# Nine taps of two convolution chunks as diagonal matrices on TensorE, a new VectorE order, and the turning inside the projection

## The chip, the cores and the metric

The kernel is one program on one core of one Trainium2 chip. The metric is the device time of one execution in microseconds; smaller is better. All inputs and outputs are 32-bit floats.

## What is computed

Four transformer layers run one after the other on a sequence of 256 positions with 1024 features: two layers of a first block, two of a second. The change touches one sublayer only, the "even mixer" of the second block's first layer, called the hybrid mixer in the kernel. Its core, from the reference:

```python
def even_mixer(h, w_in, w_out, dw_w, dw_b, ln_g, ln_b):
    """Stick-breaking attention heads || Conformer conv channels. h: (B,S,D)."""
    proj = h @ w_in
    q, k, v, u, gate = jnp.split(
        proj, [SB_WIDTH, 2 * SB_WIDTH, 3 * SB_WIDTH, 3 * SB_WIDTH + CONV_CH], axis=-1)
    a_out = merge_heads(stick_breaking_attention(
        split_heads(q, SB_HEADS), split_heads(k, SB_HEADS), split_heads(v, SB_HEADS)))
    c = u * jax.nn.sigmoid(gate)
    c = causal_depthwise_conv(c, dw_w, dw_b)
    c = jax.nn.silu(layer_norm(c, ln_g, ln_b))
    return jnp.concatenate([a_out.astype(h.dtype), c], axis=-1) @ w_out
```

There are 8 heads of 64 features and 512 convolution channels; the convolution is depthwise, causal, with 31 taps. A head's weights are `exp(log_sigmoid(z) + rest)`, where `rest` is a reversed running sum of `log_sigmoid(-z)` over the keys.

## The kernel before

**Tiling.** 128 partitions; positions come as two blocks of 128 (`NTB = 2`), features as chunks of 128. Weight slabs of 1 MB come through a ring of four slots. For a slab, SyncE loads `raw[s]`, ScalarE rounds it into `w_hi[s]` (`high_one`, L551), and VectorE, or GpSimd (L474), subtracts to get `w_lo[s]` (`low_one`, L1155, which signals `slab_ready`). A product is three passes, `three` (L1802 to L1804): hi by hi, and the two cross terms. Products whose operands are plain 32-bit floats (heads, triangles) are one call each, and stand in the trace as two MATMUL records; a transpose is one record. SyncE loads the next slab of a slot once its `slab_ready` says that `raw[s]` was read.

**Order.** Every engine has a program of its own, written out by hand, and semaphores tie them. In the hybrid mixer they are:

- TensorE: the slabs of the input projection, with heads 0 to 3 between them. The slab that gives the last keys (`slab_into(7, 3)`) is copied out by ScalarE (`evacuate(3, words(1536, 512), ..., bank=7)`, L570). Then `all_copied`, the logits of heads 4 to 7 (`stick_logits`, L2261 to L2264), values of heads 2 and 3, 18 warm matmuls on zeros (`keep_warm`, L1882), running sums of heads 4 to 7 (`stick_rest`, L2272 to L2274), 4 warm ones, values of heads 4 to 7 (`stick_values`, L2283 to L2285), 8 warm ones. Then `project_out` over chunks 0 to 3 (the heads' half; block 0, then block 1; 48 matmuls), `conv_turned` (L2293: the convolution, channels on partitions, is transposed into banks 6 and 7, positions on partitions), 16 warm ones, a wait for the layer norm, 8 transposes back (L2331), 8 warm ones, and `project_out` over chunks 4 to 7.
- VectorE: 124 taps of the convolution (4 chunks by 31; L1666 and L1669) in pieces given by `convolve(n)`, with everything else between them: `low_one`, `bounds` (L1675: a minimum of the logits, which releases ScalarE's exponential), `softplus` (L1683, which releases `stick_rest`), `low_of_banks` (L1461). After the turning: statistics (L1737), mean and variance (L1740), `1/std` (L1744), the scaling (L1746).
- ScalarE: `high_one` for the slabs, the copies out of PSUM, exp and log of a head (`softplus_logs`, L937 and L940), the weights (`stick_weights`, L947), and after the scaling SiLU (L990) and rounding (L986) of each chunk, before the second half of the output projection.

The slots 0 to 3 of the output projection hold its rows in that order: chunks 0 to 3 need slots 0 and 1, chunks 4 to 7 need slots 2 and 3.

Of the kernel before, what the change touches and what calls it, by code (L numbers as in the profile page):

```python
# [23 lines left out]
ACT = mybir.ActivationFunctionType  # L24
# [21 lines left out]
TOP_K = 64  # L46
SB_HEADS = 8
CONV_TAPS = 31
GATE_RANK = 16
GLA_TAU = 16.0  # L50
SOFTPLUS_EDGE = 20.0
CONV_CHUNKS = 4
TAPS_AHEAD, TAPS_BETWEEN = 64, 8
BUCKETS = 32
MAX_DIST = 128
# [77 lines left out]
def build(nc, A, out):  # L133
    with ExitStack() as ctx:
# [3 lines left out]
        def sem(name):  # L138
            return ctx.enter_context(nc.semaphore(name))
# [39 lines left out]
        def words(a, n):  # L179
            return arena[:, a:a + n]  # L180
# [44 lines left out]
        def col(name, i=0):  # L225
            c = row_of[name] + i
            return cols[:, c:c + 1]
# [44 lines left out]

        sb_z, sb_min, sb_ln, sb_sp, sb_rest, sb_w, sb_pv = (
            sem("sb_z"), sem("sb_min"), sem("sb_ln"), sem("sb_sp"), sem("sb_rest"), sem("sb_w"), sem("sb_pv"))
        cv_tap, cv_turn, cv_ms, cv_std, cv_norm, cv_back, cv_silu = (
            sem("cv_tap"), sem("cv_turn"), sem("cv_ms"), sem("cv_std"), sem("cv_norm"), sem("cv_back"), sem("cv_silu"))
        stored = sem("stored")
# [52 lines left out]
        def hyb_views():  # L330
            return dict(
                q=words(0, 1024).rearrange("p (c t) -> p c t", t=SEQ), k_all=words(1024, 1024),
                k=words(1024, 1024).rearrange("p (c t) -> p c t", t=SEQ),
                gate=words(3072, 1024).rearrange("p (s c t) -> p s c t", s=2, t=SEQ),
                v=proj[:, 8:10, :], pad=words(5120, 4 * (SEQ + CONV_TAPS - 1)).rearrange("p (c t) -> p c t", c=4),
                co=words(6400, 1024).rearrange("p (c t) -> p c t", t=SEQ), cs=words(7424, 1024).rearrange("p (c t) -> p c t", t=SEQ),
                l=words(8448, 1536).rearrange("p (b n) -> p b n", b=4),
                sp=words(9984, 1536).rearrange("p (b n) -> p b n", b=4), w=words(11520, 1536).rearrange("p (b n) -> p b n", b=4))

        def halves(t, m):  # L340

# [127 lines left out]
        def _(pool):  # L469
# [62 lines left out]
            for s, n in ((0, 3), (1, 3), (2, 1), (3, 4)):  # L532
                ring.skip(s, n)
            low_one(2)
            ring.skip(2, 2)
            ffn_elsewhere(3)


# [1 line left out]
        def _(act):  # L540
# [12 lines left out]
            def high_one(slot, dmas=1):  # L553
                high(slot, *ring.take(slot, dmas))
# [12 lines left out]
            def evacuate(s, dst, scale=1.0, func=ACT.Copy, bank=None):  # L567

                act.wait_ge(slab_used[s], ring.uses[s] + 1)
                ins = act.activation(dst, ps[:, 4 + s if bank is None else bank, :], func, scale=scale).then_inc(proj_free[s], 1)  # L570
                made[s] += 1
                return ins

            def preload(func, at=154):

                act.activation(small[:, at:at + 1], eps_col, func)
# [335 lines left out]
            for l in range(2):  # L912
# [13 lines left out]
                if l == 0:  # L926
# [40 lines left out]
                    evacuate(2, words(512, 512), bank=6)  # L967
                    stick_weights(1)
                    high_one(2)
                    evacuate(3, words(1536, 512), 64 ** -0.5, bank=7)  # L970
                    softplus_logs(2, 2)
                    stick_weights(2)
                    stick_weights(3)
                    high_one(3)
                    act.wait_ge(sb_pv, SB_HEADS)
                    for b in range(2):
                        act.activation(x_hi[:, 2 * b:2 * b + 2, :].rearrange("p c t -> p (c t)"), ps[:, 4 + b, :], ACT.Copy)\
                            .then_inc(x_hi_done, 1)
                    preload(ACT.Sqrt)
                    act.wait_ge(cv_ms, 1)  # L980
                    act.activation(ln_std, ln_mv.rearrange("p (b s) -> p b s", s=2)[:, :, 1], ACT.Sqrt, bias=eps_col)\
                        .then_inc(cv_std, 1)
# [55 lines left out]
        def _(dve):  # L1038
# [112 lines left out]
            def low_one(slot):  # L1151

                u, _ = lows.take(slot)
                dve.wait_ge(hi_done[slot], u + 1)
                dve.tensor_tensor(w_lo[slot][:, :], raw[slot][:, :], w_hi[slot][:, :].bitcast(F32), ALU.subtract)\  # L1155
                    .then_inc(slab_ready[slot], 1)
# [476 lines left out]
            for l in range(2):  # L1633
                ffn(False, 0, 2 + 2 * l)
                after_ffn(2 + 2 * l, ("norm_g_2", l * 6 + 2), True, 2 if l == 0 else None)
                if l == 0:
# [15 lines left out]
                        dve.wait_ge(proj_free[u_slot], made[u_slot] + 1)  # L1652

                    last_tap = {}
                    taps = [(k, 2 * half + c) for half in range(2) for k in range(CONV_TAPS) for c in range(2)]

                    def convolve(n):
                        for _ in range(n):
# [27 lines left out]
                    def bounds(pair):  # L1686
                        stick_bound(2 * pair)
                        stick_bound(2 * pair + 1)
# [25 lines left out]
                        made[s] += 1  # L1714
                    convolve(CONV_TAPS * 2 - (3 + 2 + 9 + 7 + 6 + 5 + 12))
                    gated_half(1, 0, 1)
                    low_one(0)
                    low_one(1)
                    convolve(16)
                    low_one(2)  # L1720
                    bounds(2)
                    bounds(3)
                    convolve(11)
                    softplus(2)
                    softplus(3)
                    convolve(16)
                    low_of_banks(2)
                    convolve(CONV_CHUNKS * CONV_TAPS)
                    low_one(3)
                    for s in (2, 3):  # L1730
                        used[s] += 2
                        made[s] += 2
                    dve.wait_ge(cv_tap, CONV_CHUNKS * CONV_TAPS)

                    dve.wait_ge(cv_turn, 1)
                    for tb in range(NTB):
                        ins = dve.bn_stats(ln_stats[:, 6 * tb:6 * tb + 6], ps[:, 6 + tb, :])  # L1737
# [7 lines left out]
                    for tb in range(NTB):  # L1745
                        dve.tensor_scalar(xn[:, tb, 0:512], ps[:, 6 + tb, :], ln_mv[:, 2 * tb:2 * tb + 1], ln_rstd[:, tb:tb + 1],  # L1746
                                          ALU.subtract, ALU.mult).then_inc(cv_norm, 1)
                    for c in range(4):
                        dve.wait_ge(x_hi_done, want(x_hi_done))
                        dve.tensor_tensor(x_lo[:, 4 + c, :], hyb["cs"][:, c, :], x_hi[:, 4 + c, :].bitcast(F32), ALU.subtract)\  # L1750
                            .then_inc(x_ready, 1)
# [44 lines left out]
        def _(pe):  # L1796
# [437 lines left out]
            for l in range(2):  # L2234
                turn_block(0)
                if l == 0:
# [40 lines left out]
                    def stick_values(hd):  # L2277
# [7 lines left out]
                        pe.matmul(o[:, P:SEQ], v1, w[:, SEQ:3 * P], start=False, stop=True, skip_group_check=True)\  # L2285
                            .then_inc(sb_pv, 1)

                    def conv_turned():

                        pe.wait_ge(cv_tap, CONV_CHUNKS * CONV_TAPS)  # L2290
                        for tb in range(NTB):
                            for c in range(4):
                                ins = pe.transpose(ps[:, 6 + tb, c * P:c * P + P], hyb["co"][:, c, tb * P:tb * P + P], ident)  # L2293
                        ins.then_inc(cv_turn, 1)

# [16 lines left out]
                    heads(stick_logits, 2)  # L2312
                    heads(stick_logits, 3)
                    heads(stick_values, 1)
                    keep_warm(18)
                    heads(stick_rest, 2)
                    heads(stick_rest, 3)
                    keep_warm(4)
                    heads(stick_values, 2)
                    heads(stick_values, 3)  # L2320
                    keep_warm(8)

                    base = x_new(6)
                    project_out(HYB_OUT, lambda tb, k: base + k // 2 + 1, ks=range(4))
                    conv_turned()
                    keep_warm(16, 4)
                    pe.wait_ge(cv_norm, NTB)
                    for c in range(4):
                        for tb in range(NTB):
# [58 lines left out]
```

## Time and profile before

| | |
|---|---|
| runs | 1711.65, 1714.98 (median), 1716.35 us |
| the profiled execution | 1709.17 us, span 1707.4 us |
| mean granted TensorE clock | 0.994 of full speed |
| busy | TensorE 97%, VectorE 70%, ScalarE 51%, GpSimd 7% |

All times below are microseconds from the start of the span. The hybrid mixer lies between about 884 and 997. A timeline row gives start, length (for several instructions together from the first start to the last end), engine, line, operation, tiles and count; brackets give the idle time before it and what ended it. The length of a matmul's record contains the pipeline, so that matmuls in a row overlap: the pace is read from start to start.

### The profile page before, as it was taken

How to read it: one execution, taken by the hardware profiler on the slowest of the kernel's cores; microseconds unless marked ns; L12 is line 12 of the kernel's file. 1: busy time of each engine (PE TensorE's matmuls, PEld its weight loads, DVE VectorE, ACT ScalarE, POOL GpSimd, SP SyncE). 2: the span in 40 equal slices, each digit the busy share in tenths (PEclk: the TensorE clock that was granted, in tenths of full speed). 3: DMA queues.
4: the chain of work that ended last, by engine and by line, in shares of the span. 5: the costliest groups of instructions: out<-in, count | busy, mean ns of one | idle time of the engine just before them, and what ended most of it. 6: DMA issues, size and time to landing. Idle time of an engine off the chain costs nothing. (4 is left out here: it accounts for less than half of the span.)

```text
span 1707.4 us, 26142 instructions
## 1 busy us (share of the span) xinstructions
PE 1654.7 (97%) x10075; PEld 1454.3 (85%) x10084; DVE 1197.4 (70%) x1773; ACT 863.0 (51%) x1207; POOL 116.1 (7%) x36
## 2 busy tenths in 40 slices
PE   7999999989999998999999999999999999999998
PEld 6998988879798887888889788888988889888887
DVE  2796778777668788566669966667666675676665
ACT  6323655563665556544466374446544465364443
POOL 5351000012600000000010000000000000000000
PEclk9999999999999999999999999999999999999999
DMA  8623366745245555555644235555555653345552
GB/s 267 217 75 100 124 216 192 222 133 164 69 152 173 197 177 192 161 197 173 220 148 161 94 113 177 195 184 185 174 183 196 199 182 128 124 136 177 192 189 82
DMA packets 220065, 283.44 MB, mean 166 GB/s; under 512 B 13004, under 2 KB 197315, under 8 KB 219987
## 3 DMA queue, kind: packets, MB, share of 16 engines
q1 hardware_dynamic: 218499, 278.18, 50.1%
q10 hardware_dynamic: 1488, 4.17, 0.8%
q8 instruction: 55, 0.90, 0.2%
q14 instruction: 23, 0.19, 0.0%
HBM read 280.88 MB, written 1.44 MB: 165 GB/s over the span
## 5 line engine op out<-in xcount | busy, mean ns | idle before, releaser
L1971 PE MATMUL ps<-x_pair,w_hi 128*128 128x512 f32 x1728 | 612.1, 398 | 0.0
L551 ACT ACTIVATE w_hi<-raw 128x2048 fp32r<-128x2048 f32 x262 | 498.2, 1909 | 132.9 <-PE ps L1973 92.2
L1234 DVE TENSOR_TENSOR w_lo<-raw,w_hi 128x2048 fp32r<-128x2048 f32 x162 | 371.1, 2291 | 195.4 <-ACT w_hi L551 195.4
L1973 PE MATMUL ps<-x_pair,w_lo 128*128 128x256 f32 x1728 | 485.1, 281 | 0.0
L1971 PEld LDWEIGHTS ps<-x_pair,w_hi 128*128 128x128 f32 x1728 | 324.7, 188 | 80.2
L1973 PEld LDWEIGHTS ps<-x_pair,w_lo 128*128 128x128 f32 x1728 | 326.3, 189 | 2.1
L1802 PE MATMUL ps<-w_hi,x_pair 128*128 128x256 f32 (+2 forms) x672 | 215.8, 321 | 19.6 <-DVE x_pair L1090 10.9
L1804 PE MATMUL ps<-w_hi,x_pair 128*128 128x256 f32 (+2 forms) x672 | 210.7, 314 | 0.0
L1803 PE MATMUL ps<-w_lo,x_pair 128*128 128x256 f32 (+2 forms) x672 | 210.6, 313 | 0.0
L1155 DVE TENSOR_TENSOR w_lo<-raw,w_hi 128x2048 fp32r<-128x2048 f32 x74 | 171.9, 2331 | 38.0 <-ACT w_hi L551 37.9
L1802 PE MATMUL ps<-w_hi,g_hi 128*128 128x512 f32 x480 | 188.7, 393 | 0.0
L1804 PE MATMUL ps<-w_hi,g_lo 128*128 128x512 f32 x480 | 187.7, 391 | 0.0
L1803 PE MATMUL ps<-w_lo,g_hi 128*128 128x512 f32 x480 | 187.2, 390 | 0.0
L1802 PE MATMUL ps<-x_pair,w_hi 128*128 128x256 f32 (+1 forms) x640 | 183.5, 287 | 2.5 <-POOL w_lo L474 2.2
L1803 PE MATMUL ps<-x_pair,w_hi 128*128 128x256 f32 (+1 forms) x640 | 181.6, 284 | 0.0
L1804 PE MATMUL ps<-x_pair,w_lo 128*128 128x256 f32 (+1 forms) x640 | 181.5, 284 | 0.0
L1802 PEld LDWEIGHTS ps<-w_hi,x_pair 128*128 128x128 f32 x672 | 129.6, 193 | 31.3 <-issue 14.2
L1261 DVE TENSOR_REDUCE arena<-ps 128x256 f32<-128x512 f32 x216 | 142.0, 684 | 12.3 <-PE ps L1973 10.0
L474 POOL TENSOR_TENSOR w_lo<-raw,w_hi 128x2048 fp32r<-128x2048 f32 x21 | 100.1, 4784 | 743.4 <-ACT w_hi L551 743.4
L1804 PEld LDWEIGHTS ps<-w_hi,x_pair 128*128 128x128 f32 x672 | 129.7, 193 | 7.1
L1803 PEld LDWEIGHTS ps<-w_lo,x_pair 128*128 128x128 f32 x672 | 129.9, 193 | 6.7
L1802 PEld LDWEIGHTS ps<-x_pair,w_hi 128*128 128x128 f32 (+1 forms) x640 | 122.6, 192 | 5.5 <-POOL w_lo L474 2.8
(181 smaller groups left out, 1847.2 us busy)
## 6 DMA issues: line engine op xcount, KB each, us to landing
raw<-in_ffn_w_in SPq DMA_DIRECT2D x88, 1024.0 KB, 5.1
raw<-in_ffn_w_up SPq DMA_DIRECT2D x44, 1024.0 KB, 5.1
raw<-in_ffn_w_out SPq DMA_DIRECT2D x44, 1024.0 KB, 4.9
raw<-in_ffn_w_down SPq DMA_DIRECT2D x22, 1024.0 KB, 5.3
raw<-in_hgrn_w_in SPq DMA_DIRECT2D x16, 1024.0 KB, 5.8
raw<-in_gla_w_in SPq DMA_DIRECT2D x12, 1024.0 KB, 5.3
raw<-in_hyb_w_in SPq DMA_DIRECT2D x10, 1024.0 KB, 5.5
raw<-in_dsa_w_in SPq DMA_DIRECT2D x6, 1024.0 KB, 5.7
```

The costliest lines, as they stand in the source:

```text
L474: pool.tensor_tensor(w_lo[slot][:, :], raw[slot][:, :], w_hi[slot][:, :].bitcast(F32), ALU.subtract)\
L551: act.activation(w_hi[slot][:, :], raw[slot][:, :], ACT.Copy).then_inc(hi_done[slot], 1)
L1155: dve.tensor_tensor(w_lo[slot][:, :], raw[slot][:, :], w_hi[slot][:, :].bitcast(F32), ALU.subtract)\
L1234: dve.tensor_tensor(w_lo[slot][:, :], raw[slot][:, :], w_hi[slot][:, :].bitcast(F32), ALU.subtract)\
L1261: dve.tensor_reduce(ff_u[:, b, g, :], halves_of, AX_X, ALU.add).then_inc(part_sum[g][b], 1)
L1802: pe.matmul(out_ap, a_hi, b_hi, start=start, stop=False, skip_group_check=True)
L1803: pe.matmul(out_ap, a_hi, b_lo, start=False, stop=False, skip_group_check=True)
L1804: return pe.matmul(out_ap, a_lo, b_hi, start=False, stop=stop, skip_group_check=True)
L1971: pe.matmul(ps[:, bank, :].rearrange("p (x t) -> p x t", x=2), w_hi[s][:, at:at + P], x_pair[:, :, k, :], start=k == 0, stop=False, skip_g ...
L1973: ins = pe.matmul(ps[:, bank, 0:SEQ], w_lo[s][:, at:at + P], x_hi[:, k, :], start=False, stop=k == NK - 1, skip_group_check=True)
```

## The change

Of the 31 taps, the last nine (k = 22 to 30) of channel chunks 2 and 3 go to TensorE. ScalarE writes 18 matrices of 128 by 128, the identity times a column of tap weights (`diag`, in free words of `arena`). TensorE multiplies a window of `pad` by each, for both blocks, straight into banks 6 and 7, which is where the turned convolution goes: the stationary operand is [channels, positions], the moving one the diagonal matrix, so the product comes out turned. These 36 products stand in three of the places of warm matmuls. `conv_turned` then adds VectorE's share of chunks 2 and 3 by a product with the identity, and transposes chunks 0 and 1; it stands inside the first half of the output projection, ahead of block 1, chunk 1. VectorE does 106 taps. Its two subtractions for slots 0 and 1 stand behind `bounds` of heads 4 to 7; that for slot 2 goes to GpSimd, which waits for the last tap; that for slot 3 stands behind the layer norm's scaling. ScalarE's rounding of slot 3 stands behind the copies of the heads' output.

```diff
+PE_TAPS = 9
+VECTOR_TAPS = CONV_CHUNKS * CONV_TAPS - 2 * PE_TAPS
+PE_TAP_LIST = [(k, c) for k in range(CONV_TAPS - PE_TAPS, CONV_TAPS) for c in (2, 3)]
...
@@ GpSimd
-            ring.skip(2, 2)
+            ring.skip(2, 1)
+            pool.wait_ge(cv_tap, VECTOR_TAPS)
+            low_one(2)
@@ ScalarE
                     stick_weights(1)
                     high_one(2)
+                    for j, (k, c) in enumerate(PE_TAP_LIST):
+                        act.activation(hyb["diag"][:, j, :], ident, ACT.Copy, scale=col("conv_dw_w_2", k * 4 + c))\
+                            .then_inc(diag_done, 1)
                     evacuate(3, words(1536, 512), 64 ** -0.5, bank=7)
...
-                    high_one(3)
                     act.wait_ge(sb_pv, SB_HEADS)
...
                     preload(ACT.Sqrt)
+                    high_one(3)
@@ VectorE
-                    taps = [(k, 2 * half + c) for half in range(2) for k in range(CONV_TAPS) for c in range(2)]
+                    taps = [(k, 2 * half + c) for half in range(2) for k in range(CONV_TAPS - half * PE_TAPS) for c in range(2)]
...
                     gated_half(1, 0, 1)
+                    convolve(24)
+                    bounds(2)
+                    bounds(3)
                     low_one(0)
                     low_one(1)
-                    convolve(16)
-                    low_one(2)
-                    bounds(2)
-                    bounds(3)
-                    convolve(11)
+                    lows.skip(2, 1)
                     softplus(2)
                     softplus(3)
-                    convolve(16)
+                    convolve(12)
                     low_of_banks(2)
                     convolve(CONV_CHUNKS * CONV_TAPS)
-                    low_one(3)
...
-                    dve.wait_ge(cv_tap, CONV_CHUNKS * CONV_TAPS)
                     dve.wait_ge(cv_turn, 1)
... (behind the scaling, L1746)
+                    low_one(3)
@@ TensorE
+                    def conv_taps(n):
+                        for _ in range(n):
+                            j, (k, c) = diagonals.pop(0)
+                            pe.wait_ge(diag_done, j + 1)
+                            for tb in range(NTB):
+                                pe.matmul(ps[:, 6 + tb, c * P:c * P + P], hyb["pad"][:, c, k + tb * P:k + tb * P + P],
+                                          hyb["diag"][:, j, :], start=j == 0, stop=False, skip_group_check=True)
...
-                        pe.wait_ge(cv_tap, CONV_CHUNKS * CONV_TAPS)
+                        pe.wait_ge(cv_tap, VECTOR_TAPS)
                         for tb in range(NTB):
-                            for c in range(4):
+                            for c in (2, 3):
+                                pe.matmul(ps[:, 6 + tb, c * P:c * P + P], hyb["co"][:, c, tb * P:tb * P + P], ident,
+                                          start=False, stop=True, skip_group_check=True)
+                            for c in range(2):
                                 ins = pe.transpose(ps[:, 6 + tb, c * P:c * P + P], hyb["co"][:, c, tb * P:tb * P + P], ident)
...
                     heads(stick_values, 1)
-                    keep_warm(18)
+                    conv_taps(11)
                     heads(stick_rest, 2)
                     heads(stick_rest, 3)
-                    keep_warm(4)
+                    conv_taps(4)
                     heads(stick_values, 2)
                     heads(stick_values, 3)
-                    keep_warm(8)
+                    conv_taps(3)
+                    keep_warm(2, 0)
...
-                    project_out(HYB_OUT, lambda tb, k: base + k // 2 + 1, ks=range(4))
-                    conv_turned()
-                    keep_warm(16, 4)
+                    project_out(HYB_OUT, lambda tb, k: base + k // 2 + 1, {(1, 1): conv_turned}, range(4))
+                    keep_warm(8, 4)
                     pe.wait_ge(cv_norm, NTB)
```

## Rows read from the trace of the kernel before

**Rows 1.** The page's part 1: busy us (share of the span) xinstructions of each engine.
```profile
PE 1654.7 (97%) x10075; PEld 1454.3 (85%) x10084; DVE 1197.4 (70%) x1773; ACT 863.0 (51%) x1207; POOL 116.1 (7%) x36
```

**Rows 2.** TensorE's timeline, 965 to 987: first projection half, turning, warm matmuls, second half.
```profile
965.93 1.67 PE L1882 MATMUL ps<-const 128*128 128x512 bf16 x7 [0.16 <-issue]
967.82 0.47 PE L1802 MATMUL ps<-w_hi,x_pair 128*128 128x512 f32 x1 [0.22 <-DVE x_pair L1461]
...
978.82 1.03 PE L2293 MATMUL ps<-const,arena 128*128 128x128 f32 x8
979.91 3.40 PE L1882 MATMUL ps<-const 128*128 128x512 bf16 x15
983.69 1.09 PE L2331 MATMUL ps<-const,xn 128*128 128x128 f32 x8 [0.38 <-DVE xn L1746]
984.62 1.89 PE L1882 MATMUL ps<-const 128*128 128x512 bf16 x8
986.31 0.47 PE L1802 MATMUL ps<-w_hi,x_pair 128*128 128x512 f32 x1
```

**Rows 3.** VectorE's timeline, 966 to 984: heads' low parts, last taps, the layer norm.
```profile
966.99 1.28 DVE L1461 TENSOR_TENSOR x_pair<-ps,x_pair 128x512 fp32r<-128x512 f32 x2
968.19 7.60 DVE L1669 SCALAR_TENSOR_TENSOR arena<-arena,cols 128x256 f32<-128x256 f32 x19
...
979.96 1.29 DVE L1737 BATCH_NORM_STATS2 small<-ps 128x6 f32<-128x512 f32 x2 [1.97 <-PE ps L2293]
...
982.10 1.53 DVE L1746 TENSOR_SCALAR xn<-ps,small 128x512 f32<-128x512 f32 x2
```

**Rows 4.** TensorE's timeline, 938 to 964: logits, values, warm matmuls, running sums.
```profile
947.93 0.67 PE L2261 MATMUL ps<-arena 64*128 64x256 f32 x2 [0.89 <-ACT arena L570]
...
953.21 0.71 PE L2264 MATMUL ps<-const 128*128 128x128 f32 x4
953.85 0.43 PE L2283 MATMUL ps<-arena 128*64 128x128 f32 x2
...
955.16 3.83 PE L1882 MATMUL ps<-const 128*128 128x512 bf16 x17 [0.16 <-issue]
959.40 0.70 PE L2272 MATMUL ps<-arena,const 128*128 128x256 f32 x2 [0.41 <-DVE arena L1683]
...
963.01 1.03 PE L1882 MATMUL ps<-const 128*128 128x512 bf16 x4
963.97 0.43 PE L2283 MATMUL ps<-arena 128*64 128x128 f32 x2
```

**Rows 5.** ScalarE's timeline: around the copy of the last keys.
```profile
941.72 1.91 ACT L551 ACTIVATE w_hi<-raw 128x2048 fp32r<-128x2048 f32 x1
947.08 0.60 ACT L570 ACTIVATE arena<-ps 128x512 f32<-128x512 f32 x1 [3.45 <-PE ps L1804]
```

**Rows 6.** ScalarE's timeline, 999 to 1001: scaled copies of 128 columns from PSUM.
```profile
999.04 2.17 ACT L627 ACTIVATE x_pair<-ps,cols 128x128 fp32r<-128x128 f32 x8 [1.31 <-PE ps L1890]
```

**Rows 7.** The same line of ScalarE over the span: duration ns min/median/max, first and last start.
```profile
L627 ACT ACTIVATE x_pair<-ps,cols x184: 343/382/482, 11.3 to 1520.8; 128x128 fp32r<-128x128 f32 x176, 128x256 fp32r<-128x256 f32 x8
```

**Rows 8.** TensorE's timeline, 72 to 77: 32 records of 32-bit products in a row.
```profile
72.94 3.74 PE L2053 MATMUL ps<-arena 128*128 128x128 f32 x32
76.43 0.36 PE L1802 MATMUL ps<-w_hi,x_pair 128*128 128x256 f32 x1
```

**Rows 9.** VectorE's timeline, 938 to 955: slots 0 and 1, the last bound.
```profile
938.18 4.50 DVE L1155 TENSOR_TENSOR w_lo<-raw,w_hi 128x2048 fp32r<-128x2048 f32 x2
...
953.96 0.56 DVE L1675 TENSOR_SCALAR arena<-ps 128x384 f32<-128x384 f32 x1 [0.93 <-PE ps L2264]
```

**Rows 10.** GpSimd's timeline: its one subtraction in this mixer.
```profile
890.68 4.61 POOL L474 TENSOR_TENSOR w_lo<-raw,w_hi 128x2048 fp32r<-128x2048 f32 x1 [429.74 <-ACT w_hi L551]
```

**Rows 11.** Stretches behind the mixer: busy time and records of each engine, clock, DMA.
```profile
998.00:1001.00 3.00, 1.87 (x13) 1.69 (x14) 2.14 (x7) 1.96 (x8) 0.00 (x0) 0.95 0.00 0
1001.00:1004.00 3.00, 3.00 (x16) 3.00 (x16) 2.96 (x10) 2.97 (x7) 0.00 (x0) 0.50 0.00 0
```

More of the change, by code:

```diff
@@ L274, in build @@
             sem("sb_z"), sem("sb_min"), sem("sb_ln"), sem("sb_sp"), sem("sb_rest"), sem("sb_w"), sem("sb_pv"))
+        diag_done = sem("diag_done")
         cv_tap, cv_turn, cv_ms, cv_std, cv_norm, cv_back, cv_silu = (
@@ L337, in hyb_views @@
                 l=words(8448, 1536).rearrange("p (b n) -> p b n", b=4),
-                sp=words(9984, 1536).rearrange("p (b n) -> p b n", b=4), w=words(11520, 1536).rearrange("p (b n) -> p b n", b=4))
+                sp=words(9984, 1536).rearrange("p (b n) -> p b n", b=4), w=words(11520, 1536).rearrange("p (b n) -> p b n", b=4),
+                diag=words(13056, 2 * PE_TAPS * P).rearrange("p (j n) -> p j n", n=P))
         def halves(t, m):
@@ L2286, in stick_values @@
                             .then_inc(sb_pv, 1)
+                    diagonals = list(enumerate(PE_TAP_LIST))
+                    def conv_taps(n):
[5 more added lines that the diff above has]
+                                          hyb["diag"][:, j, :], start=j == 0, stop=False, skip_group_check=True)
                     def conv_turned():
-                        pe.wait_ge(cv_tap, CONV_CHUNKS * CONV_TAPS)
+                        pe.wait_ge(cv_tap, VECTOR_TAPS)
                         for tb in range(NTB):
-                            for c in range(4):
+                            for c in (2, 3):
+                                pe.matmul(ps[:, 6 + tb, c * P:c * P + P], hyb["co"][:, c, tb * P:tb * P + P], ident,
+                                          start=False, stop=True, skip_group_check=True)
+                            for c in range(2):
                                 ins = pe.transpose(ps[:, 6 + tb, c * P:c * P + P], hyb["co"][:, c, tb * P:tb * P + P], ident)
```

## The prediction

> **What bounds the kernel now.** I read the page's head first: TensorE is busy for 97% of the span [rows 1], at a mean clock of 0.994. So a change is worth what it takes out of TensorE's own row of work, or out of its waits, and what it puts in counts in full. The page's chain of waits explains too small a share of the span to help here, so I went to the timelines of the one stage that the diff touches, first TensorE's, then the engines that release it.
>
> Two things are to be seen in TensorE's timeline at the end of the mixer [rows 2]. The first half of the output projection runs from 967.82 to 978.82 without a gap: 48 matmuls in 11.00 us, 0.229 each. The turning follows, 1.09 us to the next start. Then TensorE does nothing useful from 979.91 to 983.69 (3.78 us of warm matmuls and a short wait), because the layer norm must first be made: VectorE starts its statistics at 979.96 and has the scaled block at 982.10 + 1.53 = 983.63 [rows 3]. From the transposes back (983.69) to the second half (986.31) it is another 2.62 us, which the change leaves alone. VectorE had the last tap done at 968.19 + 7.60 = 975.79 [rows 3], 3.0 us before TensorE came to the turning. The taps do not hold the turning at its present place; they would, at 974.7, if it stood 18 matmuls earlier. That is why the taps and the turning move together.
>
> Earlier in the stage TensorE is held once by ScalarE (the copy of the last keys at 947.08, after which the logits start at 947.93) and once, by 0.41 us, by VectorE's softplus at 959.40 [rows 4, 5].
>
> **The change part by part.** I count along TensorE from the logits of head 4 to the transposes back, since there each step starts when the one before is issued.
>
> *The 18 diagonal matrices on ScalarE.* They stand behind the rounding that ends at 941.72 + 1.91 = 943.63 and ahead of the copy of the last keys. ScalarE was idle for 3.45 us there [rows 5]: that is their cover. Their price isn't in the trace. The nearest row is the scaled copy of 128 columns: 8 in 2.17 us with a record of 0.38 at the end, so (2.17 - 0.38) / 7 = 0.256 from start to start [rows 6, 7]. [...] From below: the rounding of 2048 columns out of SBUF takes 1.91 [rows 5], 0.12 for every 128 columns. I take 0.256, the row of the same size with a scale by partition: 18 x 0.256 = 4.6 us, so the copy begins at about 948.2 in place of 947.08, **+1.1 us**. Ends: 0.12 gives 2.2 us, inside the cover, and 0.0; the record's whole length of 0.38, if nothing overlapped, gives 6.8 us and +3.4, but the row itself overlaps, so I weigh this end little. What is queued behind the matrices on ScalarE is this copy and then the exponentials, and TensorE's `all_copied` waits for the copy, so the logits are late by all of it: their start goes to 949.0.
>
> The row says 0.256 for a copy with a scale from a column. The Trainium skill, ScalarE: Activation LUTs, section "What ACT_TABLE_LOAD costs", says that an ACTIVATE with immediates takes 186 ns + 0.833 ns per element, that each pointer operand adds about 93 ns, and that neighbours overlap by about 93 ns. As an estimate from that page one matrix is 186 + 93 + 107 - 93 = 293 ns, 18 are 5.3 us, and the sum below would be 0.7 us higher. It speaks against the change, but only by that much.
>
> *Bounds and softplus on VectorE.* The last bound is at 953.96 and waits for TensorE [rows 9], so it goes to 955.1. Its follower is now the pair of subtractions for slots 0 and 1 (4.50 us together [rows 9]), in place of 11 taps: bound done 955.6, subtractions to 960.1. Softplus is of the bound's size, 0.56, so head 4's is done at about 960.6. ScalarE's exponential and logarithm go beside that and are as late as the logits. TensorE, see the next step, comes at 961.1: its wait of 0.41 us for softplus is gone, and VectorE has 0.5 us to spare. In exchange VectorE idles: 24 taps at 7.60 / 19 = 0.40 [rows 3] end at about 947.9, and the first new bound is possible at about 950.7. This costs nothing as long as the last 8 taps are in time, which I check below.
>
> *Eleven taps in place of 18 warm matmuls.* A tap is two products of 128 x 128 x 128 in 32-bit floats, each two records. The trace has such a row with both operands in `arena`: 32 records from 72.94 to 76.43, 0.109 each [rows 8]. A tap is 4 x 0.109 = 0.436, 11 are 4.80 us. The stretch that they replace lasts from 955.16 to 959.40, 4.24 us, wait included [rows 4]. **+0.56 us**.
>
> *Four taps in place of 4 warm matmuls.* 1.74 us in place of 963.97 - 963.01 = 0.96 [rows 4]. **+0.78 us**. ScalarE's last weights are ready before that, so nothing was hidden by it.
>
> *Three taps and 2 warm matmuls in place of 8.* 1.31 + 2 x 0.22 + 0.16 of issue = 1.9 us against 967.82 - 965.93 = 1.89 [rows 2]. **0.0 us**. The copies of the heads' output and `low_of_banks` go on beside it. Today the first low part starts at 966.99, 3.0 us behind the first value product, and TensorE waits 0.22 us for it [rows 2 to 4]; VectorE will then be idle and not in the middle of taps, so this stays covered.
>
> *The turning.* Four of its eight transposes become products of two records: 12 x 0.109 = 1.31 in place of 1.09. **+0.22 us**. Does it have to wait? Adding up, the values start at 963.97 + 1.1 + 0.56 + 0.78 = 966.4 and the projection at 967.82 + 2.44 = 970.3. The turning stands behind 30 of its 48 matmuls, 30 x 0.229 = 6.9, at 977.1. VectorE starts `low_of_banks` 3.0 us behind the values as now, at 969.4, and has it done 1.28 later [rows 3], at 970.7; 8 taps of 0.40 follow, last tap 973.9. That is 3.2 us early. The 18 taps that VectorE is rid of were worth 7.2 us to it and buy TensorE nothing directly.
>
> *The layer norm behind the projection.* From the turning's first start to the statistics it was 979.96 - 978.82 = 1.14, now 1.4; the statistics start at 978.5 and the scaled block is there 3.67 us later [rows 3], at 982.2. TensorE meanwhile does the remaining 18 matmuls: 977.1 + 1.31 + 18 x 0.229 = 982.5. Here the gain is found: the norm is hidden completely. But 8 warm matmuls still stand between, 986.31 - 984.62 = 1.69 us [rows 2], and they run although the block is ready. So the stretch of 3.78 us becomes 1.7. **-2.1 us**, not -3.8.
>
> *Slot 2 on GpSimd, slot 3 late.* GpSimd's subtraction takes 4.61 [rows 10], from 973.9 to 978.5; slot 3 on VectorE runs from 982.2 to 984.4. Both are needed only by the second half, after 986: cover of 2 us and more. SyncE's next loads for slots 0 and 1 are let go some 17 us later than now, at 958 and 960, and those for 2 and 3 at 978 and 984.4; the feed-forward part rounds slots 0 and 1 after 987, and slots 2 and 3 after 1002. A slab lands in some 5 us, so none of them is late. **0.0 us**; if this cover failed, a late slab would cost its overhang directly.
>
> *Sum.* 1.1 + 0.56 + 0.78 + 0.0 + 0.22 - 2.1 = **+0.6 us**, on the profiled execution's 1709.17: 1709.8. The profiled execution is 5.8 us under the median of the three runs; the stage's terms do not depend on that, so I put them on the median: 1714.98 + 0.6 = **1715.6 us**. The bounds of the matrices alone move it from -0.5 to +4.0, where the upper end holds no overlap on ScalarE at all.
>
> **The rivals.**
> *A, the clock falls once more.* TensorE's gap ahead of the logits grows from 0.89 to 2.0 us. Behind the mixer a stretch of 3 us in which TensorE is busy for only 1.87 us stands ahead of one of 3 us at a granted clock of 0.50, that is 1.2 GHz instead of 2.4 [rows 11]. If the same happens at the logits, a stretch of 3 us does the work of 1.5: +1.5, together +2.1 us, 1717.1. Against it: the mean clock of 0.994 leaves room for 0.006 x 1707.4 / 0.5 = 20 us at half clock in the whole span, so that such stretches are few; and the one at 1001 could as well vanish by a shift.
>
> *B, a net gain.* The matrices stay inside the 3.45 us of cover (0.19 each decides), the logits start as now: -0.5. If besides the 3 us at 0.50 behind the mixer do not come, another -1.5: -2.0 us, 1713.0. For it: the shift changes the moment of that gap. That it would be more is excluded by the 8 warm matmuls and the 1.3 us that the taps add on TensorE in any case.
>
> *C, slower beyond the bound.* The taps don't run at 0.109 a record but like the logits' short products, which read `const` on both sides: 4 records from 953.21 to 953.85, 0.16 each [rows 4]. The windows of `pad` start at any word, which no row of the trace shows for a stationary operand. Then 72 + 8 records cost 80 x 0.051 = 4.1 us more, all on TensorE's row: +4.7 us, 1719.7, and with matrices of 0.30 (5.4 us, +0.8 on the taken value) +5.5, 0.32%. It decides from about 0.16 a record on. Against it: the row of 32 is the same kind of product, on the same tile.
>
> *D, the turning waits for the last tap.* For this VectorE would have to be 3.2 us later than worked out; it has no new work in that stretch. 2 in 100.
>
> **How the numbers follow.** Forecast 0.55, A 0.18, B 0.18, C 0.07, D 0.02. About 0.3% (5.1 us) is what a measurement of this kernel can tell from no change. All cases but part of C and D lie within it, and the before runs themselves spread over 4.7 us, which can carry a small difference across: faster 0.04, same 0.90, slower 0.06. The range takes B and C with some of the scatter of the runs: 1710 to 1721 us.
>
> **What would show it right or wrong.** In the profile of the changed kernel: 18 copies on ScalarE at about 0.26 from start to start, and the copy of the last keys behind them without an idle time; a gap of about 2 us ahead of the first logits; taps at 0.109 a record; no wait of TensorE at the turning; a second projection half that starts within 1 us of 986.3. The prediction is wrong if the taps run slower than 0.12 a record, if a wait for VectorE stands ahead of the running sums or the turning, if the gap at the scaled block is larger than the 8 warm matmuls, or if the stretches of low clock differ in number.

## The result and the profile after

The changed kernel takes 1722.1 us in the median of 20 runs (1715.88 to 1724.35), the one before 1715.4 us (20 runs, 1709.15 to 1718.66). The ratio is 1.0035, with a 95% interval of 1.0024 to 1.0045: **slower by 0.35%, some 6 us**. The forecast was +0.6 us, 1715.6, in a range of 1710 to 1721; the median lies 1.1 us above that range.

I begin with the stretches of TensorE's timeline in which the two differ. The views by stretches give busy time and records of TensorE, its weight loads, VectorE, ScalarE and GpSimd, then the granted clock and the DMA share and rate. The kernel before:

```profile
944.00:956.00 12.00, 10.95 (x74) 9.00 (x74) 10.60 (x22) 3.53 (x6) 0.00 (x0) 1.00 0.62 203
956.00:968.00 12.00, 11.22 (x74) 7.34 (x74) 12.00 (x30) 9.42 (x14) 0.00 (x0) 1.00 0.01 3
```

The changed kernel (all of its stage is some 5 us later in this execution; see the experiment before_again for that):

```profile
944.00:956.00 12.00, 9.42 (x73) 8.76 (x69) 8.63 (x22) 8.53 (x22) 0.00 (x0) 1.00 0.01 1
956.00:968.00 12.00, 12.00 (x53) 9.91 (x52) 6.09 (x6) 5.29 (x10) 0.00 (x0) 0.57 0.03 7
```

The clock is the news: 0.57 in the mean from 956 to 968, that is at 0.50 (1.2 GHz) for 10.2 us in the record of the clock. TensorE is "busy" for the whole of it, yet issues only 53 records in place of 74 (the kinds of work in the two windows are not all the same; like rows are compared below). TensorE's timeline of the changed kernel, the answer to rows 4:

```profile
954.62 0.67 PE L2268 MATMUL ps<-arena 64*128 64x256 f32 x2 [2.58 <-ACT arena L577]
...
956.09 0.70 PE L2268 MATMUL ps<-arena 64*128 64x256 f32 x2
956.62 0.38 PE L2269 MATMUL ps<-arena 64*128 64x128 f32 x2
956.93 1.16 PE L2271 MATMUL ps<-const 128*128 128x128 f32 x4
958.02 1.22 PE L2268 MATMUL ps<-arena 64*128 64x256 f32 x2
...
960.74 1.22 PE L2268 MATMUL ps<-arena 64*128 64x256 f32 x2
...
963.47 0.69 PE L2290 MATMUL ps<-arena 128*64 128x128 f32 x2
...
965.43 6.04 PE L2302 MATMUL ps<-arena 128*128 128x128 f32 x44
971.31 0.60 PE L2279 MATMUL ps<-arena,const 128*128 128x256 f32 x2
```

The first head of these logits takes 956.09 - 954.62 = 1.47 us, the third 960.74 - 958.02 = 2.72: the clock falls in the second. Ahead of the first stands the idle gap of 2.58 us, where [rows 4] had 0.89. ScalarE's timeline shows what made it (answering [rows 5]): 18 matrices from 948.52 to 953.78, 0.29 apart and not 0.256, and the copy of the last keys right behind them, without idle time:

```profile
946.72 1.91 ACT L558 ACTIVATE w_hi<-raw 128x2048 fp32r<-128x2048 f32 x1
948.52 5.37 ACT L978 ACTIVATE arena<-const,cols 128x128 f32<-128x128 f32 x18
953.78 0.58 ACT L577 ACTIVATE arena<-ps 128x512 f32<-128x512 f32 x1
```

At the end of the stage everything is as forecast. VectorE (answering [rows 3]) has its last tap at 980.38 + 3.25 = 983.63 and waits 5.03 us for the turning, not the other way round, and the block is ready at 990.80 + 1.53 = 992.3; TensorE (answering [rows 2]) issues the rest of the first half until 992.81 and then 8 warm matmuls that nobody needs:

```profile
980.38 3.25 DVE L1679 SCALAR_TENSOR_TENSOR arena<-arena,cols 128x256 f32<-128x256 f32 x8
988.65 1.30 DVE L1743 BATCH_NORM_STATS2 small<-ps 128x6 f32<-128x512 f32 x2 [5.03 <-PE ps L2313]
...
990.80 1.53 DVE L1752 TENSOR_SCALAR xn<-ps,small 128x512 f32<-128x512 f32 x2
```

```profile
992.81 1.67 PE L1889 MATMUL ps<-const 128*128 128x512 bf16 x7
994.33 1.04 PE L2351 MATMUL ps<-const,xn 128*128 128x128 f32 x8
```

**One ledger for all traces.** I measured the same six stretches on TensorE in every trace, from start to start, from the values of head 0 (one slab of the input projection before the gap) to the second half of the output projection. The table is worked out from the timelines; "hold" runs to the logits of head 4, and the last stretch contains the turning, the norm and the transposes back.

| kernel | hold | logits | to the sums | to the values | to the projection | to the 2nd half | total |
|---|---|---|---|---|---|---|---|
| before | 9.73 | 5.92 | 5.55 | 4.57 | 3.85 | 18.49 | 48.1 |
| before_again | 9.73 | 5.92 | 5.54 | 4.57 | 3.85 | 18.46 | 48.1 |
| changed | 11.42 | 8.85 | 7.84 | 5.40 | 3.41 | 16.77 | 53.7 |
| after_again | 11.43 | 9.90 | 8.35 | 5.39 | 3.42 | 16.79 | 55.3 |
| fill | 11.44 | 5.93 | 6.09 | 5.39 | 3.41 | 16.79 | 49.1 |
| early | 9.73 | 5.93 | 6.08 | 5.40 | 3.41 | 16.80 | 47.4 |
| held | 11.42 | 8.81 | 6.79 | 4.46 | 3.31 | 18.55 | 53.3 |
| hold_15 | 10.55 | 5.92 | 6.09 | 5.39 | 3.42 | 16.80 | 48.2 |
| taps_only | 9.73 | 5.93 | 6.09 | 5.39 | 3.41 | 18.99 | 49.5 |
| turn_only | 9.73 | 5.93 | 5.53 | 4.58 | 3.85 | 15.76 | 45.4 |
| early_trim | 9.77 | 5.93 | 6.09 | 5.39 | 3.41 | 15.06 | 45.7 |
| seven | 9.74 | 5.92 | 5.59 | 4.60 | 3.42 | 15.06 | 44.3 |

The change adds 53.7 - 48.1 = 5.6 us to the stage in the profiled execution, which at 1723.8 us is one of the slower of the 20; the times say some 6 us. What is open at this point is why the clock falls.

### The profile page after: what moved, and what is told of

It reads as the page before. It is cut to its first block and busy times, and to the rows that moved or that the text cites. A ratio compares the mean times of both kernels' runs of the same rounds, so it can differ in the third digit from the quotient of the medians.

```text
span 1722.0 us, 26222 instructions
## 1 busy us (share of the span) xinstructions
PE 1666.7 (97%) x10116; PEld 1469.3 (85%) x10124; DVE 1189.3 (69%) x1754; ACT 868.3 (50%) x1225; POOL 120.6 (7%) x37
## 3 DMA queue, kind: packets, MB, share of 16 engines
q1 hardware_dynamic: 218499, 278.18, 49.5%
## 5 line engine op out<-in xcount | busy, mean ns | idle before, releaser
L1809 PE MATMUL ps<-w_hi,x_pair 128*128 128x256 f32 (+2 forms) x672 | 218.8, 326 | 19.1 <-DVE x_pair L1100 10.6
L1811 PE MATMUL ps<-w_hi,x_pair 128*128 128x256 f32 (+2 forms) x672 | 213.3, 317 | 0.0
L479 POOL TENSOR_TENSOR w_lo<-raw,w_hi 128x2048 fp32r<-128x2048 f32 x22 | 104.6, 4773 | 831.8 <-ACT w_hi L558 748.4
L1809 PEld LDWEIGHTS ps<-w_hi,x_pair 128*128 128x128 f32 x672 | 131.8, 196 | 30.5 <-issue 13.1
L1811 PEld LDWEIGHTS ps<-w_hi,x_pair 128*128 128x128 f32 x672 | 132.0, 196 | 7.4
```

What stands on the lines that cost most here:

```text
L479: pool.tensor_tensor(w_lo[slot][:, :], raw[slot][:, :], w_hi[slot][:, :].bitcast(F32), ALU.subtract)\
L1809: pe.matmul(out_ap, a_hi, b_hi, start=start, stop=False, skip_group_check=True)
L1811: return pe.matmul(out_ap, a_lo, b_hi, start=False, stop=stop, skip_group_check=True)
```

## The experiments

**The changed kernel again, for a second trace.** No edit.

> The changed kernel unaltered, for a second trace of it. Theory 'clock': the granted clock is 0.50 for about 10 us from the logits of head 4 on again, and the ratio is 1.003 to 1.004 again. Rival 'chance': the fall at that place was the luck of one execution; then this trace has full clock between the logits and the running sums, and the loss has to be looked for elsewhere.

Ratio 1.0026 (1.0012 to 1.0040), a little under the 1.003 to 1.004 that I expected. The fall is there again, after the same gap of 2.58 us, and lasts 13.7 us this time; the stage takes 55.3 us. It is not the luck of one execution. This trace too is of one of the longer executions (1722.8 us), and whether all executions have the fall, two traces can't say; the times are looked at under hold_15.

**The gap filled with warm matmuls.**

```diff
                     slab_into(7, 3)
+                    keep_warm(10, 0)
                     all_copied()
                     heads(stick_logits, 2)
```

> The changed kernel with 10 warm matmuls into bank 0 between the last slab of keys and the wait for its copy, so that TensorE isn't idle for the 2.6 us ahead of the logits; nothing waits longer (10 x 0.216 = 2.2 us). Theory 'clock': the clock stays at 1.0 through logits and taps, the stage is some 4 to 5 us shorter than in the changed kernel, ratio to before 1.000 to 1.001. Rival 'work': the taps and VectorE's order cost the time themselves; then the ratio stays at 1.003 or above.

Ratio 1.0007 (0.9997 to 1.0016). TensorE's timeline:

```profile
952.54 2.33 PE L1889 MATMUL ps<-const 128*128 128x512 bf16 x10
955.30 0.67 PE L2268 MATMUL ps<-arena 64*128 64x256 f32 x2 [0.43 <-ACT arena L577]
...
961.23 0.43 PE L2290 MATMUL ps<-arena 128*64 128x128 f32 x2
...
962.30 5.18 PE L2302 MATMUL ps<-arena 128*128 128x128 f32 x44
967.32 0.60 PE L2279 MATMUL ps<-arena,const 128*128 128x256 f32 x2
```

The logits start as late as in the changed kernel, 11.44 us after the values of head 0, but they run at full clock, and the stage is 4.6 us shorter than the changed kernel's and 6.2 us shorter than its second trace. Ten matmuls that compute nothing take back nearly all of the loss. The 18 matrices stand in their old place here and hold the copy as long, so they do no harm of their own beyond the hold. "Clock" holds, "work" falls.

**The matrices made early.** `diagonals(n)` makes the next n of the 18 (its definition is left out).

```diff
                     high_one(3)
                     for s in range(2):
                         evacuate(s, hyb["v"][:, s, :], bank=s)
                         high_one(s)
+                    diagonals(9)
                     evacuate(2, words(0, 512), bank=6)
                     high_one(2)
+                    diagonals(9)
                     evacuate(3, words(1024, 512), 64 ** -0.5, bank=7)
...
                     high_one(2)
-                    for j, (k, c) in enumerate(PE_TAP_LIST):
-                        act.activation(hyb["diag"][:, j, :], ident, ACT.Copy, scale=col("conv_dw_w_2", k * 4 + c))\
-                            .then_inc(diag_done, 1)
                     evacuate(3, words(1536, 512), 64 ** -0.5, bank=7)
```

> The changed kernel with the 18 matrices made some 35 us earlier on ScalarE, 9 ahead of and 9 behind the copy of the second query slab, in its idle times there. The copy of the last keys is then on time, and TensorE's gap ahead of the logits is 0.9 us as before the change. Theory 'clock': no fall there, and the 1.7 us of the hold are gone too: ratio 0.999 to 1.000. Rival 'work': ratio 1.002 to 1.003, only the hold's 1.7 us less than the changed kernel.

Ratio 0.9992 (0.9982 to 1.0001), the stage at 47.4. Hold and fall are both gone. This is what the parts of the change are worth without them: 48.1 - 47.4 = 0.7 us in the trace. The times alone can't tell it from the kernel before, since the interval reaches 1.0001.

**Only the hold: the kernel before, with the matrices made in the changed kernel's place and not used.** The constants, the semaphore and the tile that this needs are left out of the cut.

```diff
                     stick_weights(1)
                     high_one(2)
+                    for j, (k, c) in enumerate(PE_TAP_LIST):
+                        act.activation(hyb["diag"][:, j, :], ident, ACT.Copy, scale=col("conv_dw_w_2", k * 4 + c))\
+                            .then_inc(diag_done, 1)
                     evacuate(3, words(1536, 512), 64 ** -0.5, bank=7)
```

> The kernel before with the 18 matrices made on ScalarE at the changed kernel's place, and used by nobody: only the hold of the copy. Theory 'clock': TensorE's gap ahead of the logits is 2.6 us, the clock falls at the logits, but the 18 warm matmuls behind them bring it back sooner than the taps do: 1.7 us for the hold and 2 to 4 us for the clock, ratio 1.002 to 1.003. Rival 'the taps pull the clock down': full clock here, +1.7 us alone, ratio 1.001.

Ratio 1.0034 (1.0021 to 1.0048) from six runs, above the 1.002 to 1.003 that I expected, and as much as the whole change. The stretches:

```profile
944.00:956.00 12.00, 9.42 (x77) 8.79 (x74) 12.00 (x19) 8.52 (x22) 0.00 (x0) 1.00 0.54 176
956.00:968.00 12.00, 12.00 (x46) 8.59 (x47) 6.20 (x14) 4.86 (x9) 0.00 (x0) 0.57 0.27 88
```

And TensorE's timeline:

```profile
955.11 0.67 PE L2268 MATMUL ps<-arena 64*128 64x256 f32 x2 [2.58 <-ACT arena L574]
...
963.92 0.69 PE L2290 MATMUL ps<-arena 128*64 128x128 f32 x2
...
965.89 4.98 PE L1889 MATMUL ps<-const 128*128 128x512 bf16 x18
970.71 0.59 PE L2279 MATMUL ps<-arena,const 128*128 128x256 f32 x2
```

The same gap, the same fall of 10.2 us, without a tap on TensorE and with all warm matmuls in place. So neither the taps nor the missing warm matmuls pull the clock down. That the 18 warm ones would end the fall sooner than the taps did not show: it lasts 10.2 us here, 10.2 and 13.7 us in the two traces with taps. Its price was lower, though: of 53.3 - 48.1 = 5.2 us the hold is 1.7, which leaves 3.5 us for the fall, within the 2 to 4 expected, against 4.7 in the changed kernel.

**The hold without the gap: the same kernel with 10 warm matmuls ahead of the wait.** The edits are those of held and of fill together.

> The kernel before with the 18 unused matrices in the changed kernel's place on ScalarE, and the 10 warm matmuls into bank 0 ahead of the wait: the hold without the idle gap. Theory 'clock': full clock at the logits, and what is left is the hold alone, +1.7 to 2.1 us, ratio 1.001. Rival 'the matrices hurt otherwise' (by a shared port, or the table reload): ratio stays at the 1.0034 of the held kernel.

Ratio 1.0005 (0.9995 to 1.0014). The hold of 1.7 us alone would be 1.0010, inside the interval; the fall is needed for the 1.0034. There is no trace of this kernel that can be compared; that the clock stays up here rests on the times, and on the mean clocks of the runs, 0.990 to 0.992 against 0.985 to 0.989 in held.

**The kernel before again, for a second trace.** No edit.

> The kernel before unaltered, for a second trace of it: which of the stretches of low clock outside the mixer are its own. Ratio 1.000, and its interval says what this comparison can tell apart. All theories of the mixer expect full clock between the slab of the last keys and the running sums.

Ratio 0.9995 (0.9985 to 1.0006). The stage takes 48.1 us as in the first trace, though it begins 5.1 us later in the span (values of head 0 at 943.28 in place of 938.20). The record of the clock has more low stretches ahead of the mixer here than in the first trace, and they lie at the same places as in the traces of the changed kernel. So the 5 us by which the changed kernel's stage is later in its profile are none of the change's doing, and the two profiled executions, 1709.17 and 1723.8 us, exaggerate the difference. The prediction wanted to be called wrong if the stretches of low clock differ in number; that sign says nothing, since they differ between two traces of one kernel (five in the first, six in this).

**Fifteen matrices in place, three early: a gap in between.**

```diff
+                    diagonals(3)
                     evacuate(2, words(0, 512), bank=6)
                     high_one(2)
...
                     high_one(2)
-                    for j, (k, c) in enumerate(PE_TAP_LIST):
-                        act.activation(hyb["diag"][:, j, :], ident, ACT.Copy, scale=col("conv_dw_w_2", k * 4 + c))\
-                            .then_inc(diag_done, 1)
+                    diagonals(15)
                     evacuate(3, words(1536, 512), 64 ** -0.5, bank=7)
```

> The changed kernel with 15 of its 18 matrices in their place and 3 made early: the copy of the last keys is held by some 0.8 us in place of 1.7, TensorE's gap ahead of the logits is about 1.7 us, between the 0.9 without a fall and the 2.6 with one. If the gap's length alone decides and 1.7 us is short enough: full clock there, ratio 1.000 to 1.001. If it is long enough: the fall of 10 us again, ratio 1.002 to 1.003. Falls in some executions only would show as two clusters of times.

Ratio 1.0007 (0.9998 to 1.0016).

```profile
954.11 0.67 PE L2274 MATMUL ps<-arena 64*128 64x256 f32 x2 [1.70 <-ACT arena L577]
```

After 1.70 us of gap the clock stays up in this trace. Of 12 runs ten lie at 1714.8 to 1717.2 us and two at 1721.1 and 1721.8, with mean clocks of 0.988 and 0.986 against 0.989 to 0.992 in the ten: as if the fall came in some executions at this length. It is not shown: neither of the two has a trace, and fill, which has no such gap, has one run of this kind as well (1721.3 us, 0.988).

The changed kernel's own 20 runs form two groups, seven from 1715.9 to 1718.8 (mean clocks 0.987 to 0.990) and 13 from 1720.8 to 1724.4 (0.985 to 0.987); in after_again five lie at 1715.7 to 1718.6 and six at 1720.2 to 1724.2. All three traces that show the fall (the two of this kernel and that of held, 1724.3 us) are of executions above 1722 us. So it may well be that the faster executions do not have it. But the kernel before has two groups too, 1709.2 to 1712.0 and 1714.7 to 1718.7, and no trace of a faster execution of the changed kernel was taken: likely, not shown.

That one and the same gap does not always bring a fall is shown elsewhere in these traces. Some 20 us behind the stage stands a gap of 2.09 us ahead of eight transposes, for example at 1017.41 in the changed kernel's first trace and at 1019.46 in its second. The clock is at 0.50 for 3.4 us behind it in the first and stays at 1.00 in the second, though the program is the same. Of the eleven traces whose gap there is 2.08 to 2.10 us, six show a fall at its end or up to 1.5 us behind it (before_again, changed, early, held, turn_only, seven) and five do not (after_again, fill, hold_15, taps_only, early_trim). And in the first trace of the kernel before, the clock fell at 1001 [rows 11] behind gaps of only 1.14 and 0.54 us.

**Only the taps: matrices early, the turning back behind the projection half.**

```diff
-                    project_out(HYB_OUT, lambda tb, k: base + k // 2 + 1, {(1, 1): conv_turned}, range(4))
-                    keep_warm(8, 4)
+                    project_out(HYB_OUT, lambda tb, k: base + k // 2 + 1, ks=range(4))
+                    conv_turned()
+                    keep_warm(16, 4)
```

> The kernel with the matrices made early and the turning back behind the first projection half, with 16 warm matmuls ahead of the wait, as before the change: the taps on TensorE and VectorE's order alone. Theory 'the taps are a cost, the turning's place the gain': from the first logits to the transposes back 37.1 us (before the change 35.8, with the turning inside 35.0), +1.3 us in all, ratio 1.0008. Rival 'the taps themselves bring the gain': 35.8 or less, ratio below 1.000.

Ratio 1.0005 (0.9996 to 1.0013), the stage at 49.5, 1.4 us above before (expected: 1.3). By the trace the taps on TensorE, taken alone, are a cost; in the times it is too small to tell from nothing.

**Only the turning: the kernel before, with it moved.** All 124 taps stay on VectorE, and slot 3's subtraction goes behind the scaling as in the change; the turning stands one chunk later than in the change, so that the last tap is just in time.

```diff
-                    project_out(HYB_OUT, lambda tb, k: base + k // 2 + 1, ks=range(4))
-                    conv_turned()
-                    keep_warm(16, 4)
+                    project_out(HYB_OUT, lambda tb, k: base + k // 2 + 1, at={(1, 2): conv_turned}, ks=range(4))
+                    keep_warm(4, 4)
...
                     convolve(CONV_CHUNKS * CONV_TAPS)
-                    low_one(3)
...
                         dve.tensor_scalar(xn[:, tb, 0:512], ps[:, 6 + tb, :], ln_mv[:, 2 * tb:2 * tb + 1], ln_rstd[:, tb:tb + 1],
                                           ALU.subtract, ALU.mult).then_inc(cv_norm, 1)
+                    low_one(3)
```

> The kernel before with the turning alone moved into the first projection half, ahead of block 1, chunk 2, with 4 warm matmuls in place of 16 and slot 3's subtraction behind the scaling; all 124 taps stay on VectorE, no matrices. The last tap at about 975.8 comes just ahead of the turning at 976.1. 12 matmuls, 2.75 us, hide part of the layer norm. Theory 'the turning's place is the gain, the taps on TensorE are a cost': -2.7 us, ratio 0.9984. Rival 'the turning needs the taps off VectorE': TensorE waits for the last tap and the ratio is 0.9995 or above.

Ratio 0.9986 (0.9974 to 0.9998), the stage at 45.4: -2.7 us, as expected.

```profile
983.10 1.03 PE L2293 MATMUL ps<-const,arena 128*128 128x128 f32 x8
986.71 1.04 PE L1882 MATMUL ps<-const 128*128 128x512 bf16 x4
987.97 1.09 PE L2330 MATMUL ps<-const,xn 128*128 128x128 f32 x8 [0.22 <-DVE xn L1745]
```

The turning comes without a wait (no bracket), VectorE's 19 last taps, begun at 975.20, being done at 982.82. The change's gain can be had without any of its cost.

**The eight needless warm matmuls taken out.** The kernel early, without `keep_warm(8, 4)` ahead of the wait for `cv_norm`.

> The kernel with the matrices made early, and without the 8 warm matmuls ahead of the wait for the scaled block. Theory: the block is ready 0.5 us before TensorE has issued the first half, so the 1.7 us of warm matmuls are pure loss: ratio 0.998, some 1.7 us under the early kernel's. Rival: the clock falls without them at the second half and gives 1.5 us or more back; then the ratio is 0.999 or above.

Ratio 0.9975 (0.9965 to 0.9985), the stage at 45.7, 1.7 us under early. The transposes back start behind the last matmul without a wait for VectorE, and the clock stays up:

```profile
982.18 0.38 PE L2319 MATMUL ps<-const,arena 128*128 128x128 f32 x2
986.53 1.04 PE L2356 MATMUL ps<-const,xn 128*128 128x128 f32 x8
```

**Seven taps in place of nine.** The edit is to early_trim; the two `diagonals(9)` become `diagonals(7)`.

```diff
-PE_TAPS = 9
+PE_TAPS = 7
...
-                    convolve(24)
+                    convolve(28)
...
-                    conv_taps(11)
+                    conv_taps(9)
...
-                    conv_taps(4)
+                    conv_taps(2)
```

> The early_trim kernel with seven taps of two chunks on TensorE in place of nine: 9, 2 and 3 taps in the three places in place of 11, 4 and 3, 28 of VectorE's 110 taps ahead of the bounds in place of 24, 14 matrices. Two taps less in the first place save 0.56 us until the wait for softplus takes over, two less in the second 0.8 us; VectorE's taps still end ahead of the turning. Theory 'every tap on TensorE counts in full there': 1.2 us under early_trim, ratio 0.9968. Rival: softplus, the weights or the last tap take the place; ratio as early_trim's, 0.9975 or above.

Ratio 0.9977 (0.9968 to 0.9987), 1711.85 us. In the trace the stage is shorter by another 1.3 us (44.3), at the two places where I expected it: 0.50 to the sums, 0.79 to the values. The times can't tell it from early_trim: I expected 0.9968, which is the end of the interval, and the rival's 0.9975 lies inside it. Both kernels are faster than the kernel before and the changed one.

## Why the prediction was wrong

**The parts at full clock were right.** The kernel fill shows them without the fall. By the steps of the prediction:

| step | forecast | measured |
|---|---|---|
| matrices hold the copy of the last keys | +1.1 | +1.7 |
| 11 taps for 18 warm matmuls | +0.56 | +0.54 |
| 4 taps for 4 | +0.78 | +0.82 |
| 3 taps and 2 warm for 8 | 0.0 | -0.44 |
| turning, norm, transposes back | +0.22 - 2.1 | -1.7 |
| sum | +0.6 | +0.9 |

Hold: I took 0.256 for a matrix from a row that reads PSUM; they came at (953.78 - 948.52) / 18 = 0.29. The prediction's estimate from the Trainium skill, ScalarE: Activation LUTs, section "What ACT_TABLE_LOAD costs", was 293 ns, and the trace agrees with it; the hold by that estimate, 1.1 + 0.7 = +1.8, is close to the +1.7 measured. The taps ran at 5.02 / 44 = 0.114 a record in fill, against 0.109 from [rows 8] and 0.16 in rival C; whatever their windows, which start at any word, cost is within those 0.005. In the third place the taps began 1.73 us behind the start of the values in fill, where the warm matmuls had begun after 1.96 [rows 2, 4], and the wait of 0.22 us for the first low part is gone. Rival B is out, since the matrices came at 0.29 and not within 0.19, and so is rival D: VectorE's last tap was 3.5 us ahead of the turning in the changed kernel (983.63 against 987.12). The prediction said that the 8 remaining warm matmuls were a loss of 1.7 us, and the stage of early_trim is shorter by just that. One sum of the prediction is wrong: with the matrices at +3.4 in place of +1.1 the forecast moves to +2.9 us, not to +4.0. The measured loss is beyond both.

**The step that failed is the clock: the sum has no term for a fall at the logits.** It stands only as rival A, and that was wrong in its size and in its chance. Rival A named the place and the cause: the longer gap at the logits, and a clock of 0.50 after it. But it put the fall at 3 us and its price at +1.5, and gave it 18 in 100. It lasted 10.2 and 13.7 us; the logits took 2.92 and 3.97 us longer than at full clock, the values and taps behind them 1.75 and 2.26: +4.7 and +6.2 us in the two traces (the first two stretches behind the hold, against fill). With the full-clock parts of +0.9 that is the measured 5.6 and 7.2. I had sized it by the one stretch of 3 us at 0.50 behind the mixer [rows 11], which is followed by the long matmuls of a projection; the same trace has one of 6.8 us, from 14 to 21 us, where TensorE begins its work, and I did not use it. Here the logits follow, short products of 32-bit floats, and the clock did not come back during them, though TensorE was recorded as busy without a pause. That the kind of work makes the fall so long is not shown.

The chance was low for two reasons. I took the gap as 2.0 us; with the matrices at 0.29 it was 2.6, and the gaps measured here are 0.9 (no fall in seven traces), 1.7 (none in one trace) and 2.6 (a fall in all three traces that have it); but see above for the gap of 2.09 us, which has a fall behind it in about half of the traces. And I argued from the mean clock that such stretches are few, which counts the stretches and says nothing of a place with a new gap.

**What is not settled:** what besides the gap decides whether the clock falls, since the same gap does and does not bring it about elsewhere; in what share of the changed kernel's executions it falls here; and what makes the fall last 10 or 14 us. The kernel held rules out the taps as the cause of the fall, but no run separates the logits' part in its length. The loss in the times, 6.0 us with an interval of 4.1 to 7.7, needs no further cause: the traces give 5.6 and 7.2 with the fall, and if only the 13 slower of the 20 runs had it, the mean would be an estimated 0.9 + 13/20 x (4.7 to 6.2) = 4.0 to 4.9.

## What to carry to other kernels

Work put ahead of a copy that TensorE waits for is to be priced twice: by the time that it holds the copy, and by what the longer gap can do to the clock of the products behind it; here, where the clock fell, the second was some three times the first. Put such work into idle time further up, or fill the gap with warm matmuls, and take warm matmuls out where the work that they bridged has been hidden. When a change has a part that costs and a part that gains (the taps +1.4 us, the turning's place -2.7), run each alone.

## What the runs showed of the hardware

- A gap of 2.58 us on TensorE, in front of 32-bit products of 128 to 256 columns, was followed by 10.2 to 13.7 us at a granted clock of 0.50, in three traces of three, all of slower executions of their kernels; 10 warm matmuls in the gap (0.43 us left) kept it at 1.00. At 0.50 a head of logits took 2.72 us in place of 1.49, with TensorE recorded as busy throughout: the busy share does not show such a loss, the length of like rows (0.70 us for two records of 64x256, then 1.22) and the clock do.
- A gap of 2.09 us behind the stage was followed by 3.4 us at 0.50 in six traces of eleven and by no fall in five; of the two traces of the changed kernel one shows it and one does not. No length of gap can be called safe or fatal from these runs.
- The Trainium skill, TensorE: Matmul & The Clock Gate, section "The HAM clock gate (the "warmup" mystery)", says that the clock has two states, half and full, that the throttled one is the default and that activity releases it. The traces agree with the first: away from the moments of change, stretches of 1 us show 0.50 or 1.00. They add that work which fills TensorE's row need not release it soon: here not for 10.2 to 13.7 us.
- ScalarE's scaled copy of 128 columns from SBUF came every 0.29 us; the scaled copy of 128 columns out of PSUM [rows 6] came every 0.256. The two differ in the output's type too (f32 and fp32r), so that the source alone is not shown to make the difference.
